# Block 1's attention heads rebuilt: values of eight heads at once, pairs of query tiles, normalisation at the output, stream and head outputs kept in DRAM

## What is computed

```
z = h @ w_in                                  # c_q 384, c_kv 256, k_r 32, dq dk dv 3x512, gates 2x1024
q  = rms_norm(c_q) @ w_uq                     # 8 heads A of 64 + 32 (the 32 get an axial rotation)
kv = rms_norm(c_kv) @ w_ukv                   # 8 heads A: keys 64, values 64; k_r (rotated) is shared
o_a = softmax((qn kn + qr kr) * 96**-0.5) @ va             # 8 heads A
o_b = (softmax(q1 k1 /8) - lam * softmax(q2 k2 /8)) @ vb   # 4 heads B, 2 x 64 keys, values 128, rotated
o_b = rms_norm(o_b, g_sub) * (1 - lam_init)
merged = sigmoid(ga) * (o_a @ w_br_a) + sigmoid(gb) * (o_b @ w_br_b)
x = x + gate * (merged @ w_out)               # then a convolutional feed-forward part
```

## Time and profile before

| | |
|---|---|
| median of 3 runs | 4115.38 us (4113.83 to 4117.14) |
| the profiled execution | 4118.89 us, its span 4117.2 us |
| TensorE matmul busy | 3743.1 us, 91% |
| weight loads, VectorE, ScalarE, POOL busy | 72%, 44%, 34%, 12% |
| the chain that ended last | TensorE 79%, VectorE 10%, ScalarE 6% |
| mean granted clock of TensorE | 0.942 of full speed |
| transfers | 289.85 MB, 70 GB/s over the span |

### The profile page before, as it was taken

How to read it: one execution, slowest core, us unless ns; L and a number is a source line. 1 busy time by engine, 2 the same in 40 slices (tenths; PEclk the granted TensorE clock), 3 DMA queues, 4 the chain that set the end, 5 groups by cost and what they waited for, 6 DMA issues and landing times.

```text
span 4117.2 us, 43513 instructions
## 1 busy us (share of the span) xinstructions
PE 3743.1 (91%) x18338; PEld 2954.1 (72%) x18338; DVE 1827.8 (44%) x2504; ACT 1417.2 (34%) x2153; POOL 473.5 (12%) x324
## 2 busy tenths in 40 slices
PE   7788988998999998899999999878999877988997
PEld 5555766777888886567766788666888666766886
DVE  5588544114543533664422545444433455324233
ACT  4344345113432324333322423334222344243222
POOL 0133100112100110110012101112000210221001
PEclk9889988999999999999999999989999877999999
DMA  4222100111112111220112222211232200212222
GB/s 180 72 91 85 57 26 31 46 67 42 62 57 72 62 57 63 80 98 32 46 61 82 78 98 93 96 62 64 90 110 87 85 21 1 82 52 72 90 97 70
DMA packets 55044, 289.85 MB, mean 70 GB/s; under 512 B 6977, under 2 KB 14401, under 8 KB 28737
## 3 DMA queue, kind: packets, MB, share of 16 engines
q1 hardware_dynamic: 54848, 287.06, 20.5%
HBM read 284.94 MB, written 2.10 MB: 70 GB/s over the span
## 4 chain that ended last, share of the span: by engine, by line
PE 79%; DVE 10%; ACT 6%; issue 2%; POOL 2%; DMA 1%; SPq 1%; POOLq 0%; ACTq 0%; DVEq 0%
PE psum L587 21%; PE psum L588 21%; PE psum L589 21%; PE psum L579 12%; DVE arena L1148 1%; POOL arena L1559 1%; ACT arena L1059 1%; PE psum L1011 1%; DVE arena L1176 1%; ACT arena L2250 1%; PE psum L886 1%; DVE arena L1160 1%; DVE arena L777 1%; DVE arena L1205 1%; DVE split_inputs L784 1%
## 5 line engine op out<-in xcount | busy, mean ns | idle before, releaser
L587 PE MATMUL psum<-split_inputs,split_weights 128*128 128x512 f32 (+2 forms) x3080 | 1170.4, 380 | 87.3 <-DVE split_inputs L784 33.8
L588 PE MATMUL psum<-split_inputs,split_weights 128*128 128x512 f32 (+2 forms) x3080 | 1136.1, 369 | 0.0
L589 PE MATMUL psum<-split_inputs,split_weights 128*128 128x512 f32 (+2 forms) x3080 | 1134.9, 368 | 0.0
L579 PE MATMUL psum<-arena 128*64 128x128 f32 (+14 forms) x3104 | 713.0, 397 | 111.8 <-DVE arena L1176 65.9
L587 PEld LDWEIGHTS psum<-split_inputs,split_weights 128*128 128x128 f32 (+1 forms) x3080 | 587.5, 191 | 227.7 <-issue 83.6
L579 PEld LDWEIGHTS psum<-arena 128*128 128x128 f32 (+4 forms) x3104 | 439.7, 189 | 367.8 <-issue 220.7
L588 PEld LDWEIGHTS psum<-split_inputs,split_weights 128*128 128x128 f32 (+1 forms) x3080 | 589.2, 191 | 101.0 <-issue 10.8
L589 PEld LDWEIGHTS psum<-split_inputs,split_weights 128*128 128x128 f32 (+1 forms) x3080 | 587.8, 191 | 97.3
L552 DVE TENSOR_TENSOR split_weights<-arena,split_weights 128x2048 fp32r<-128x2048 f32 (+1 forms) x228 | 472.8, 2074 | 396.7 <-ACT split_weights L541 396.5
L541 ACT ACTIVATE split_weights<-arena 128x2048 fp32r<-128x2048 f32 (+1 forms) x228 | 387.5, 1699 | 128.4 <-PE psum L589 121.5
L587 PE MATMUL psum<-split_hidden,split_weights 128*128 128x512 f32 (+1 forms) x880 | 324.0, 368 | 0.0
(11 more groups left out here) (239 smaller groups left out, 4030.1 us busy)
## 6 DMA issues: line engine op xcount, KB each, us to landing
arena<-w_ada_dram SPq DMA_DIRECT2D x48, 1024.0 KB, 4.9
arena<-w_up_dram SPq DMA_DIRECT2D x44, 1024.0 KB, 4.9
arena<-ffn_up_dram SPq DMA_DIRECT2D x44, 1024.0 KB, 4.8
arena<-w_in_dram SPq DMA_DIRECT2D x28, 1024.0 KB, 4.9
arena<-w_down_dram SPq DMA_DIRECT2D x32, 704.0 KB, 4.1
arena<-ffn_down_dram SPq DMA_DIRECT2D x32, 704.0 KB, 4.1
arena<-od_w_in_dram SPq DMA_DIRECT2D x13, 1024.0 KB, 4.9
arena<-w_br_dram SPq DMA_DIRECT2D x16, 512.0 KB, 3.6
```

Source lines behind the costliest of these rows:

```text
L579: ins = pe.e.matmul(dst, a, b, start=i == 0, stop=i == n - 1)
L587: pe.e.matmul(dst, a[0], b[0], start=i == 0, stop=False)
L588: pe.e.matmul(dst, a[0], b[1], start=False, stop=False)
L589: ins = pe.e.matmul(dst, a[1], b[0], start=False, stop=i == n - 1)
```

## The change

- Scores, q, k, values, their rotation in B and the branch products all become `mm3` style products of split operands. Latents (`CQ`, `CKV`), queries, keys (`QH`, `KH`), values (`VA`, `VB`), the turned rows (`PT`) and the head outputs (`OH`) each get a high half from ScalarE and a low half from VectorE.
- `w_uq` (two blocks), `w_ukv` (one) and `w_br` (eight) go through the common raw and split slots. The block `w_uq` holds the swapped rotary columns as well, so that A's rotation is one product with a table (`turn_a`) whose lower 32 rows are summed in the scores.
- A's values are made for all eight heads at once ahead of the heads (`v_a`); B's for two heads at once inside head A7 (`v_b`).
- The item list works on pairs of query tiles and chunks of two key tiles (512 columns of turned row). A chunk's items are: scores of a tile of the next pair, turn, norm square, values of the chunk before, norm, one or more pieces of the next head, ada steps.
- Ada steps: in A one at every second chunk (layer 0) or every third (layer 1), in B three a chunk until they are used up.
- The maximum is taken negated, the scale is folded into the queries. A's rows are no longer scaled: the reciprocals are turned by a matmul (`inverse`) and the output is multiplied. B's rows are summed with lam l1 / l2 and scaled at the output too.
- Each pair's output (256 columns) is stored to DRAM (`store_o`) and read back in the merge (`load_o`, three buffers), where it is split. B's norm is made per pair.
- `VA` lies where `X` was. At the end of layer 0 `X` is stored (`store_x`); after the merge it is read back (`load_x`), in layer 0 from the input.
- The merge waits for the last outputs' scaling, no longer for B's last norm, and prepares two weight blocks a step.

The core of the diff:

```
-    for i, u in enumerate(units):
-        out.append(("scores", u))
-        out += next(ada, [])
-        out.append(("weigh", u))
-        if i > 1:
-            values(units[i - 2])
...
+    out += [("prepare",)] + [("v_a", t) for t in range(N_TOK // P)]
...
+        for c in range(pair["chunks"]):
...
+            if ahead:
+                scores(ahead.pop(0))
+            out.append(("turn", i, c))
+            late = [closed.pop()] if closed else []
+            out += [("ob_square", x) for x in late]
+            values()
+            out += [("ob_norm", x) for x in late]
+            last = (i, c)
+            for step in queue[0:at_once]:
+                out += step
+            queue = queue[at_once:]
+            slot += 1
+            for _ in range((slot % 2 if layer == 0 else slot % 3 == 0) if pair["kind"] == "A" else 3):
+                out += next(ada, [])
```

```
+                elif what == "scores":
...
+                    for sub in range(1 if p["kind"] == "A" else 2):
...
+                        dve.e.tensor_reduce(st[:, sub:sub + 1], psum[:, b:b + p["keys"]], AX.X, ALU.max, negate=True
+                                            ).then_inc(*maxed(l, t, sub))
+                    for x in waiting:
+                        weigh(x)
+                    waiting = [t] if p["kind"] == "B" else []
+                elif what == "turn":
...
+                    hi, lo = (PT[dve_chunks[i, c] % 2][:, j, :] for j in range(2))
+                    dve.wait_ge(w_half, "turn", l, i, c)
+                    dve.e.tensor_tensor(lo, banks.at("turn", l, i, c), hi.bitcast(F32), ALU.subtract).then_inc(
+                        *banks.back(("turn", l, i, c), taken, "turn", l, i, c))
```

```
-                            ins = mm(ps[:, x:y], [(QH[at, i, q0:q0 + P], KH[at, i, x:y])])
...
+                        for i, (a, b) in enumerate(three(q, k)):
+                            ins = []
+                            for sub, rows_at in enumerate(subs):
+                                dst = psum[:, score_bank(p, t, sub) * BANK + x:score_bank(p, t, sub) * BANK + y]
+                                ins.append(pe.e.matmul(dst, a[rows_at, :], b[rows_at, :], start=i == 0, stop=i == 2))
```

```
-                        mm(ps[:, 0:n], [(w_br[m % 2][:, k, g * P:(g + 1) * P], BRANCH[g][:, k, s[0]:s[1]])
-                                        for k in range(4)]).then_inc(*product("branch", l, m, s, g))
+                        o = [(OH[:, 0, 4 * g + k, s[0]:s[1]], OH[:, 1, 4 * g + k, s[0]:s[1]]) for k in range(4)]
+                        mm3(ps[:, 0:n], [(w(k, g * P, (g + 1) * P), o[k]) for k in range(4)],
+                            [(taken, "o", l, 4 * g + k) for k in range(4)]).then_inc(*product("branch", l, m, s, g))
```

More of the change, by code:

```diff
@@ L306, in pieces @@
[L306 to L316 removed]
+            steps = [[("a_q", n, h, s)] for s in streams] + [[("a_k", n, h, s)] for s in (LAT, CTX)]
+            if h == 3:
+                steps[len(streams) - 1].append(("prepare",))
@@ L318, in head_items, with values, scores @@
+        return steps
+    def values():
+        if last:
+            out.append(("values",) + last)
+            p = pairs[last[0]]
+            if p["kind"] == "B" and last[1] == p["chunks"] - 1:
+                closed.append(p["i"])
+    def scores(t):
+        if t < 2 * len(pairs):
+            out.append(("scores", t))
+    out += [("prepare",)] + [("v_a", t) for t in range(N_TOK // P)]
     for step in pieces(0):
         out += step
[L320 to L342 removed]
@@ L347, in head_items @@
+    values()
+    for i in closed:
+        out += [("ob_square", i), ("ob_norm", i)]
     for step in ada:
```

934 lines of the change are left out of this document (555 added, 379 removed).

## The result

The changed kernel takes **4276.34 us** (4274.5 to 4277.14, 4 runs) against 4114.6 for the kernel before in the same measurement: ratio 1.0387, 95% interval 1.0371 to 1.0402. It is slower, as forecast, but by 162 us and not by 35, and the time lies 51 us above the range. The profiled execution's span is 4272.8 us for 4117.2, 155.6 more.

The account below looks back on a forecast made before the run. Rings of waits between ScalarE and VectorE, not TensorE, were to set the pace: layer 0 +14, layer 1 +42, merge -19, so +37 on 4118.9 gives 4156, less 3.5, rounded 4150 us; range 4050 to 4225.

Parts of the forecast that it names:

- the 232 us of saved work: TensorE's matmuls in both layers: -118 and -114 us, the gain if TensorE sets the pace.
- The terms for A7: Head A7, where B's values and first q, k are queued: TensorE-bound, 78 us for 56 and 73 for 44.
- the merge: Merge behind the heads: fewer matmul us, less the reading back of head outputs; -19 us together.
- the first maximum: Stage ahead of the heads: the first row maximum comes 13 us later in layer 0 and 16 in layer 1.
- the new ring, A: Heads A: DVE and ACT take turns, 3.45 us a scored chunk, 26.5 us a layer 0 head, 21.1 in layer 1.
- Three weight splits, +9.5 a layer: Heads A: three weight splits fall into the ring of DVE and ACT, adding 9.5 us a layer.
- the norm: Heads B: square, ones matmul, ln, exp now run per pair, 3 for 2 a layer 0 head, 3.6 us each.
- The clock restarts: Heads B: TensorE restarts at the low clock after idling, four a layer 0 head, two in layer 1; +31, +16 us.
- TensorE as the bound: Whole kernel: ACT and DVE run far enough ahead, so TensorE sets the pace; 3915 us, chance 1 in 12.
- the hidden projections: Heads B: projections stay hidden as now, q, k waits and most restarts go; 4060 us, chance 1 in 4.
- The rival of longer rings: Ada sums on ACT wait for POOL, delaying exps in 12 chunks, more cold restarts in A; 4215 us, 1 in 8.
- The last rival: Layer 0 B: DVE instructions with two SBUF inputs wait out POOL products; +35 us, 4185 us, chance 1 in 16.

Follow-up runs that it names:

- e1: Changed kernel with two ada steps behind every chunk of heads A in layer 0 and one in layer 1, none in B; ratio 1.0218, 4212 us.
- e18: e17 with scores ahead of values in layer 0's heads A too, except over the last value product of a pair; ratio 1.0067.
- e2: Changed kernel with the two weight blocks prepared back to back at the end of head A6 taken apart, the second prepared in A7; ratio 1.0331.
- e3: Changed kernel with the heads' ada dots, products and sums cut from 1024 columns to 16, order, waits and transfers kept; ratio 1.0156.
- e8: Changed kernel with the edits of e1, e2 and e4 together; ratio 1.0096.
- e6: Changed kernel with ten throwaway matmuls in front of TensorE's wait for the first transposes of each pair in heads B; ratio 1.0309.
- e17: e8 with layer 1 A scores ahead of values, norm matmul behind values, A's value tiles behind two score tiles, one layer 1 pair without ada step; ratio 1.0062.
- e4: Changed kernel with the next head's q or k projections issued ahead of the transposes in TensorE's list in heads B; ratio 1.0239.
- e11: Changed kernel with the norm's ones matmul in B issued behind the values and any projection of the same chunk in TensorE's list; ratio 1.0309, 4245 us.
- e12: e8 with the filler matmuls of e6 and the scores ahead of the values in heads A; ratio 1.0176.

## Why the prediction was right or wrong

**The sign and the frame held.** TensorE does not set the pace: its busy time fell by 149 us and the span grew by 156, so the 232 us of saved work bought nothing. Heads B lose more than heads A win. The terms for A7 (+22 and +29, measured +20 and +28), the merge (-14, -5; -14, -0.5) and the first maximum (+13, +16; +9, +11) held within 5 us. That the last head B of layer 0 takes 40.1 us, forecast 40, is luck: I had it without ada steps, and it carries two of the dots and waits for the last products. Without steps it takes 34.3 (e1).

**The step that failed first: "the new ring, A".** I wrote that DVE and ACT take turns and that a scored chunk is 3.45 us. In layer 1 that sum gives 21.1 us a head; e9, which takes TensorE's scores from behind its value product, runs at 20.6. The changed kernel needs 24.4, because TensorE's list is in order too: the scores stand behind a value product that waits for VectorE's low half, come at a lower clock after that wait, and the next maximum waits for them. So the ring has a third link, 3.8 us in a plain head, 18 over seven. In layer 0 the shortest heads took 27.1 and 27.5, forecast 26.5, and there the third link is not shown (e18).

**"Three weight splits, +9.5 a layer."** I counted engine time. Head A6, where two stand back to back, is 15 us (layer 0) and 19 (layer 1) over the head ahead of it, and e2 took 8 and 10 of that away. The term left out is the second transfer, which waits for the raw slot. The rest of the 26 us in layer 0's A (A2 took 35.2, A3 31.0) is explained only in part: in A2 VectorE waits 3.8 us for a block of ada weights and makes the low half of a weight block, and in both heads the granted clock is 0.83, for 0.94 in the head of 27.1 us.

**B: 342 for 300 and 238 for 217.** The largest term that was too small is the ada steps. I took 1.15 us a dot and half a POOL product where the two meet, 45 us in layer 0 and 10 in layer 1, and nothing for the transfers of their weights or for ScalarE's wait. Their work cost 60 and 14 (e3); with their transfers they cost 72 and 29 (e1), which is 27 of the 43 us missing in layer 0 and 19 of the 21 in layer 1. The place fits: all eight dots of layer 1's B lie in its head B0, which takes 91.7 us (first reciprocal to last output copy) for 63.6 in e1, while B1 and B2, with none, take 61.1 each where I had 60.0 (54.7 and 5.3 of restarts). The second step that failed is the norm: I priced its chain on VectorE and ScalarE, and left out that TensorE's ones matmul waits for the square with the projection behind it. Taking it out of the way was worth 19 and 11. TensorE's projections cost 41, inside what I had, and 35 in layer 1 for 25. Each was measured alone and they share waits (e8), so they do not add up: in layer 1 these overshoot the 21, and something in my heads there was too large. The clock restarts (31 and 16) are bounded only from below, by e6's 14 and 12.

**The rivals.** TensorE as the bound and the hidden projections are out: the B heads of layer 0 took 95 us, and the second needed under 67. The rival of longer rings came nearest, 4215 for 4276, and its mechanism is there: exponentials behind a sum start 18 us late in all in layer 0's B, where it had 25. The last rival, VectorE waiting out POOL, is real too, 20 us of its 35. Both lie inside the ada steps' 60 us, and neither has the wait for their weights.

**Readings and sums of the forecast that were off.** In the first window of the earlier trace rows TensorE is busy 82% and VectorE 77%, so the range of 82 to 92% holds for all four windows. "Table loads 20 for 12" counts one load for each chain of a norm; the traces have two, 40 for 24. The terms of the bare head B (four tiles of 6.0, two of 3.6, norms 8) give 39.2, not 38, and the 54.7 of a layer 1 head B is given without its working. None of these is of size in the sum.

**What stays open.** How the 60 us of the ada steps' work divide among dots and waits for products; which term of layer 1's heads B was too large; how much of the third link in A is order and how much is clock; what else the slow heads of layer 0's A wait for; and the 0.6% by which e17 is still slower. By its profile those are A7 (+19 and +24), layer 1's A (+15), less 14 in the merge of layer 0.

## What to carry to other kernels

Three engines that each follow one common list in order are one ring, and a wait on any of them holds what stands behind it on all: before adding up two engines' turns, write down for each wait of the third what is queued behind it. A saving on the busiest engine bought nothing here once waits between the engines set the pace; then the order of its list counts (e4 and e11 moved items in TensorE's list alone, for 1.5 and 0.8 per cent). Where two uses of a staging slot stand back to back and the other slot is taken, the second costs a transfer and not one more operation (7.03 us of waiting in e2's rows). A term that fits may fit by luck: check what else is in the measured stretch.

## What the runs showed of the hardware

A VectorE instruction with two SBUF inputs, one element a partition, took 1.98 us beside a POOL product and 0.22 without. TensorE at a granted clock of 0.68 in B rose to 0.78 with ten throwaway matmuls in each of its idle times, and the kernel got 0.8% shorter; where the projections had gone ahead of those waits already (e12), B was 8 us longer with them. Six score matmuls took 2.12 us behind an idle time and 1.30 without one. Forty table loads of 1.28 us, 51 us of ScalarE's time, were worth 12 us in the profile and 19 in the median; six of them in a head without projections were worth 7.4 us there, and those in heads with projections less than 1.
